# A mixture-of-experts router on one Trainium2 core: five accumulating count products in place of fourteen, and two gathers that read their indices without a copy

## The reference

```python
def hier_moe(h, rg_w, rg_b, re_w, re_b, w_gate, w_up, w_down):
    t = h.reshape(-1, shape[-1])
    g_prob = jax.nn.softmax(t32 @ rg_w + rg_b, axis=-1)
    g_p, g_idx = lax.top_k(g_prob, 1)
    e_logits = (t32 @ re_w + re_b).reshape(n_tok, N_GROUPS, EXPERTS_PER_GROUP)
    e_sel = jnp.take_along_axis(e_logits, g_idx[:, :, None], axis=1)[:, 0]
    top_p, top_i = lax.top_k(jax.nn.softmax(e_sel, axis=-1), TOP_K)
    top_p = top_p / jnp.sum(top_p, axis=-1, keepdims=True)
    weights = g_p * top_p
    expert_id = g_idx * EXPERTS_PER_GROUP + top_i
    comb = jnp.sum(jax.nn.one_hot(expert_id, N_EXPERTS) * weights[..., None], axis=1)
    def step(acc, xs):
        wg, wu, wd, cw = xs
        y = (jax.nn.silu(t @ wg) * (t @ wu)) @ wd
        return acc + y * cw[:, None], None
    acc, _ = lax.scan(step, jnp.zeros(t.shape), (w_gate, w_up, w_down, comb.T))
    return acc

for i in range(DEPTH):                       # the second block, DEPTH = 2
    ...
    h_lat = h_lat + g1 * y                   # y: attention and pool (i = 0), gate and convolution (i = 1)
    h_lat = h_lat + g2 * hier_moe(modulate(h_lat, norm2_g[i], sh2, sc2), *moe_args)
```

## Time and profile before

| | |
|---|---|
| median of 3 runs | 2271.97 us (2271.78 to 2272.02) |
| profiled execution, its own time | 2271.2 us |
| its span, first to last instruction | 2269.6 us |
| outside the span | 1.6 us |
| PE busy | 2068.3 us, 91% |
| mean granted PE clock | 0.944 of full speed |
| router and experts of layer 0, layer 1 | from about 1507 and 2006 us to the end of the layer |

### The profile page before, as it was taken

The page is one execution under the profiler, slowest core; times in us unless marked ns, Lnnn a source line. Parts: engine busy times, 40 slices in busy tenths (PEclk is TensorE's granted clock), DMA queues, the critical chain, the costliest instruction groups (busy, mean ns, idle before and its releaser), DMA issues. The chain is left out here.

```text
span 2269.6 us, 23301 instructions
## 1 busy us (share of the span) xinstructions
PE 2068.3 (91%) x7860; PEld 1119.4 (49%) x7860; DVE 803.7 (35%) x1642; ACT 564.3 (25%) x1157; POOL 717.5 (32%) x1059
## 2 busy tenths in 40 slices
PE   7999999999999999999987979987997799868995
PEld 5555555554554455555532546554443344354442
DVE  1444444432124343433215278342222401342223
ACT  3234331233224343222412016311110111001110
POOL 4766666766776677400000040001111000001101
PEclk9999999999999999999998889977999799868997
DMA  7234334234333333541213310054995420064994
GB/s 294 86 111 165 130 128 137 84 118 155 126 133 111 137 135 123 191 187 47 112 65 120 135 37 1 1 206 157 368 368 208 166 87 11 0 265 167 370 366 169
DMA packets 71117, 339.28 MB, mean 149 GB/s; under 512 B 8759, under 2 KB 10229, under 8 KB 56693
## 3 DMA queue, kind: packets, MB, share of 16 engines
q1 hardware_dynamic: 38502, 217.48, 25.4%
q0 software_dynamic: 27920, 103.82, 13.0%
q10 hardware_dynamic: 4608, 16.78, 1.8%
HBM read 292.97 MB, written 45.09 MB: 149 GB/s over the span
## 5 line engine op out<-in xcount | busy, mean ns | idle before, releaser
L386 PE MATMUL psA<-gB,ring 128*128 128x512 f32 x1024 | 455.1, 597 | 0.0
L324 POOL TENSOR_TENSOR wm<-wm,cs 128x256 f32<-128x256 f32 x448 | 266.7, 628 | 133.3 <-DMA wm<-in_mod_w 132.7
L386 PEld LDWEIGHTS psA<-gB,ring 128*128 128x128 f32 x1024 | 189.5, 190 | 223.8 <-issue 223.8
L328 POOL TENSOR_TENSOR wm<-wm 128x256 f32<-128x256 f32 x336 | 243.9, 754 | 30.4 <-issue 22.5
L378 PE MATMUL psA<-ring,gB 128*128 128x384 f32 (+1 forms) x768 | 243.5, 474 | 1.2 <-ACT gB L665 1.2
L1314 POOL COPY idx<-idx 128x1 int32 (+1 forms) x32 | 5.9, 183 | 711.6 <-DVEq L1907 479.1
L378 PEld LDWEIGHTS psA<-ring,gB 128*128 128x128 f32 x768 | 145.0, 191 | 92.4 <-issue 7.4
L842 DVE COPY probT<-psT 128x512 f32<-128x512 f32 x96 | 65.9, 687 | 160.7 <-PE psT L367 160.7
L1445 PE MATMUL psSO<-wreg,arena 128*128 128x512 f32 x256 | 115.3, 593 | 1.9 <-DVE arena L1929 1.9
L1430 PE MATMUL psA<-wreg,arena 128*128 128x512 f32 x256 | 116.1, 608 | 0.0
L1387 PE MATMUL psA<-wreg,mixT 128*128 128x512 f32 x256 | 112.5, 602 | 1.6 <-issue 0.8
(11 more groups left out here) (279 smaller groups left out, 2801.2 us busy)
## 6 DMA issues: line engine op xcount, KB each, us to landing
wm<-in_mod_w POOLq DMA_DIRECT2D x56, 1024.0 KB, 7.8
wreg<-in_w_gu SPq DMA_DIRECT2D x16, 2048.0 KB, 9.0
wreg<-in_w_dn SPq DMA_DIRECT2D x32, 1024.0 KB, 12.6
ring<-in_w_qk SPq DMA_DIRECT2D x24, 1024.0 KB, 4.9
mixT<-in_w_gu SPq DMA_DIRECT2D x8, 2048.0 KB, 8.7
aT<-in_w_gu SPq DMA_DIRECT2D x8, 2048.0 KB, 8.9
ys_scratch<-arena ACTq DMA_DIRECT2D x32, 512.0 KB, 9.8
ring<-in_w_v SPq DMA_DIRECT2D x8, 1536.0 KB, 6.7
```

What stands on the lines that cost most here:

```text
L324: nc.gpsimd.tensor_tensor(wm[:, b, k], wm[:, b, k], c_all[:, k].to_broadcast([P, MCH]), ALU.mult)
L328: nc.gpsimd.tensor_tensor(wm[:, b, k], wm[:, b, k], wm[:, b, n + k], ALU.add)
L386: m = nc.tensor.matmul(psA[:, n % 2, :], w(i), src[:, k, :], start=(i == 0), stop=(i == len(ks) - 1))
```

## The change

Three things are changed. The counts are made by five products that accumulate in PSUM: the moving operand is the flat `selsum` with one more block of 16 zero columns behind it, and product `s` takes its first (5 - s) blocks and adds them to the output from block `s` on. So block `t` again receives `tri` times tile `t` and `ones` times each earlier tile. DVE clears the zero block with a memset ahead of the sum, and `selsum` moves to another place in `arena`. The first two gathers take their offsets straight from `idx`, whose columns are known when the kernel is built, and the count that the later gathers wait for is two lower.

```diff
-    selsum, cnt = part(tmp_at + 128, NT, EXPERTS), part(tmp_at + 192, NT + 1, EXPERTS)
+    cnt = part(tmp_at + 192, NT + 1, EXPERTS)
+    selsum = part(tmp_at + 400 + 16 * THR, NT + 1, EXPERTS)
...
                 def gather(c, b):
                     nc.gpsimd.tensor_copy(idx1[:, b:b + 1], idx[:, ds(c, 1)]).then_inc(idx_moved[l], 1)
-                    pool.wait_ge(idx_moved[l], c + 1)
+                    pool.wait_ge(idx_moved[l], c - 1)
...
                 for b in range(2):
-                    gather(b, b)
+                    pool.indirect_dma_start(xg[:, b, :], None, d["xs"], bass.IndirectOffsetOnAxis(idx[:, b:b + 1], 0))\
+                        .then_inc(xg_loaded[l][b], 16)
...
-                for t in range(NT + 1):
-                    for s in range(min(t + 1, NT)):
-                        m = nc.tensor.matmul(psO[:, 1, t * EXPERTS:(t + 1) * EXPERTS], tri if s == t else ones[:],
-                                             selsum[:, s, :], start=(s == 0), stop=(s == min(t, NT - 1)))
+                flat_sum = selsum.rearrange("p t e -> p (t e)")
+                every = (NT + 1) * EXPERTS
+                for s in range(NT + 1):
+                    at = s * EXPERTS
+                    m = nc.tensor.matmul(psO[:, 1, at:every], ones[:] if s else tri, flat_sum[:, 0:every - at],
+                                         start=(s == 0), stop=(s == NT))
                 m.then_inc(cnt_ready, 1)
...
-                flat_sum = selsum.rearrange("p t e -> p (t e)")
+                flat_sum = selsum[:, 0:NT].rearrange("p t e -> p (t e)")
+                nc.vector.memset(selsum[:, NT, :], 0.0)
                 nc.vector.tensor_tensor(flat_sum, sel[:, 0, :], sel[:, 1, :], ALU.add).then_inc(sel_ready, 1)
```

More of the change, by code:

```diff
@@ L1089, in second_block @@
     past, chunk_hot = part(tmp_at + 400, TOP * NT, THR), part(tmp_at + 400 + 8 * THR, TOP * NT, CHUNKS)
-    assert tmp_at + 400 + 16 * THR <= 13408
+    assert tmp_at + 400 + 16 * THR + (NT + 1) * EXPERTS <= 13408
     slot_hot = part(2048, TOP * NT, P)
```

## The result

The changed kernel takes 2263.93 us (median of 6 runs, 2261.12 to 2265.4) against 2271.88 for the kernel before on the same chip (2270.17 to 2274.57). The ratio is 0.9962, with a 95% interval of 0.995 to 0.9975. It is 8.0 us faster; 8.2 were forecast. A second set gave 2264.89 against 2271.3, ratio 0.9973 (0.9961 to 0.9984). Over both sets the mean of the 13 runs is 2264.2, and that of the 50 runs of the kernel before in all sets is 2272.3. The profiled execution took 2262.04 us, with a span of 2260.4.

What follows compares the result with a forecast made beforehand. The router's chain of waits, a relay between engines, was taken as what the change could shorten, though PE is busy 91% of the span. 7.65 - 0.18 + 0.71 = 8.2 us, from 2271.97 to 2263.8 us; range 2261.0 to 2266.3.

Steps and rivals of the forecast that it cites:

- Which links count: Router: a relay of PE, DVE, POOL and gather; shortening a link shortens the kernel unless something beside it becomes late.
- Part 1, the counts: PE's router counts: 18 fewer records at 0.2125 us, price flat from 16 to 128 columns; 3.83 us a layer, 7.65 in all.
- The cover by DVE's `wts`: DVE's `wts` work beside PE's counts: the new counts still end 1.0 us after it is done.
- Part 2, the memset: DVE's memset of the zero block, on the path ahead of the sum: 0.09 us each, 0.18 us lost in all.
- Part 3, the first gather: Gap from POOL's chunk-number load to the first gather falls from 1.17 and 1.08 to 0.77 us; 0.71 us gained in all.
- The second gather: Lands 5.53 us after the first one's start; PE waits for ACT until 6.99 us anyway, so its gain is worth nothing.
- The clock: PE's clock rise at the first wide products: 0 booked, 1.7 us put on each side of the range.
- the rival of a late clock: Clock rises late at both layers' wide products: gain 4.8 us, time 2267.2 us; chance 8%.
- Columns as the price: Rival: columns set the count products' cost, counts lose 0.43 us a layer, 2272.3 us, no change; chance 2%.
- Gathers that disturb each other: Rival: the second gather's DMA, starting 1.25 us behind the first, takes bandwidth from it; 2265.2 us; chance 4%.
- A link that waits for data: Rival: counts shorten but the next link waits for data landing at 1542 us; 2267.6 us with half lost; chance 2%.
- A clock that stays low: Rival: PE stays at 1.2 GHz far into the chunks, making the kernel slower by over 4.5 us; chance 2%.

Runs made afterwards that it cites:

- the records of five widths: Changed kernel plus spare float32 products of 16, 80, 128, 192 and 256 columns in gaps where PE waits for DVE; 2258.69 us in its one run.
- the bfloat16 kernel: Changed kernel with the count products and their operands in bfloat16 instead of float32; 2260.66 us (4 runs) against 2272.22, ratio 0.9946.

## Why the prediction was right

**Which links count** was read from the chain of waits, and in the profiles each link that was shortened brought forward what stands behind it. In the timed runs only the counts can be seen: alone they gain 8.1 us, and the gathers alone nothing that the runs can tell.

**Part 1, the counts.** Forecast 3.83 us a layer, measured 3.84 in the chain. The step that did it, a price set per record and flat from 16 to 128 columns, read from two neighbouring rows, is shown directly by the records of five widths: flat to 128, and rising behind it. In the changed kernel itself the ten records start within 1.91 us, 0.212 apart on average. The cover by DVE's `wts` was forecast as 1.0 us and was 1.00; the bfloat16 kernel shows what happens when it is used up. Data for the first chunk was in time.

**Part 2, the memset.** Forecast 0.18 us lost, measured 0.10 (0.03 and 0.07). The size was off, by 0.08: it runs beside the sum.

**Part 3, the first gather.** Forecast 0.71, measured 0.72. The step was to take the gap from the gathers at a layer's end (0.77) and not to book the whole 1.1 us. The number was right and the ground for it only half: an indirect DMA that follows no other one does not always need 0.77. The rows at a layer's end stand behind a semaphore increment and the new gather behind a register load, and the gap happened to be about the same behind both (0.78 and 0.76, 0.81 and 0.72). When the DMA does the waiting itself it is 0.28 and 0.27. A row of that kind was not in the trace before.

**The second gather** was called worth nothing, and that came true, with less room than was worked out. The forecast had it land 4.28 us after its own start, as the first one does, and 5.53 after the first one's start. But the second one took 4.77 and 4.91 us already before, and now takes 5.00 and 5.49, so it lands at 6.34 and 6.74, which is level with ACT in layer 1. The turn link fell by 0.05 and 0.22 us (0 and 0.25 in the second profile). Less the landing of the first gather it is 4.58 us in both kernels, both layers and all three profiles, so this is the first gather landing sooner. The runs do not show that the change did that: with the gathers alone changed it landed after 4.34 and 4.35 us.

**The clock** was booked at 0, with 1.7 us on each side. Its share in the first pair of profiles is 1.2 us gained and 0.3 lost; in the second pair 0.16 and 1.22 gained. So each of the four lies within its bounds, but that the median came within 0.2 us of the forecast is partly luck: the second set of the same kernel gave 6.4 us. The Trainium skill, "TensorE: Matmul & The Clock Gate", section "Part 1: The HAM clock gate", says that the number of slow products at a start differs between executions of one kernel; two profiles of the same kernel, 7.42 and 8.46 us in layer 0, agree. The remark that both layers had the same delay, which spoke against the rival of a late clock, was thin: the equality was one profile's. In the timed runs the kernel before spreads over 2269.4 to 2275.6 us, so the 0.72 us of the gathers and the 0.10 of the memset are known from the links alone.

**The rivals.** Columns as the price: refuted up to 128. Gathers that disturb each other: the first still lands after 4.23 and 4.04 us, against 4.28 and 4.26; the second takes 0.2 and 0.6 us longer than before, and still lands no later than ACT is done. A link that waits for data: none. A clock that stays low: the wide products were at the full clock 4.2 us after the first one at the latest.

## What to carry to other kernels

In a relay of engines price a narrow float32 product by its record and not by its columns: at the lower clock up to 128 columns wider was free here, so merge products whose operands overlap. Before you shorten one link, look at what runs beside it, since its slack is the end of the gain (1.0 us here, used up by the bfloat16 counts). When profiles of two kernels differ, compare links whose clock is the same in both; totals hold the clock's luck as well.

## What the runs showed of the hardware that was not expected

- The same code ahead of every edit brought the logits of layer 0 at 1525.25 to 1529.76 us over fourteen profiles. Counted from the kernel before, a profile is -1.6 to +0.4 us off after the first 50 us and keeps this within 0.5 us up to 1180 us. Between 1180 and 1400 us, where the clock falls and rises several times, it becomes 0 to 5 us later: this stretch held 61 us at the lower level in the kernel before, 65 where it was 0.5 to 1.2 us later, 68 where it was 1.7 to 3.7 later, and 72 where it was 5 later.
- Products that do nothing useful made the kernel faster: by 6.4 us against the changed kernel, for 30 float32 products of 512 columns in idle gaps.
- Five bfloat16 products with a new weight load each start within 0.19 us of one another (spacing 0.035 to 0.056 us, at the lower clock), where 0.107 to 0.11 had been expected from the float32 records.
- An indirect DMA started 0.27 to 0.28 us after the drain that released it when it did the waiting, 0.72 to 0.84 us behind a register load or a semaphore increment of POOL, and 0.30 behind another indirect DMA.
